# Recurrent heads summed onto all partitions and normalised one by one, with the attention halves of two output stages ahead of the head halves

## The reference, cut to what matters

```python
o = outs[0] + outs[1]                                          # forward + backward, (B, S, 4, 128)
o = o * rsqrt(mean(o * o, axis=-1) + EPS)                      # one mean per head and token
o_hgrn = o.reshape(B, S, 512) * norm_g * silu(g_raw)
mixed = concatenate([o_hgrn, o_attn], axis=-1) @ w_mix_out[l]  # 1024 -> 1024
x = x + g2[:, None, :] * mixed
h = modulate(rmsnorm(x, norm_g[l, 2]), sh3, sc3)               # then the second feed-forward
```

## Time and profile before

| | us |
|---|---|
| Median of 3 runs (lowest, highest) | 1129.79 (1128.75, 1131.01) |
| The profiled execution | 1127.93 |
| Its span in the trace | 1126.1 |
| Matmuls busy (TensorE) | 1084.9 |
| VectorE, ScalarE, GpSimd busy | 561.0, 400.4, 75.6 |
| Mean granted TensorE clock | 0.988 |

### The profile page before, as it was taken

One profiled execution on the slowest core, in us unless ns is written; L12 is line 12 of the kernel. 1 busy time (PEld: TensorE's weight loads), 2 busy tenths in 40 slices (PEclk: granted clock), 3 DMA queues, 4 the chain that ended last, 5 costly groups with the idle time before them and its releaser, 6 DMA issues.

```text
span 1126.1 us, 12577 instructions
## 1 busy us (share of the span) xinstructions
PE 1084.9 (96%) x5007; PEld 875.7 (78%) x5007; DVE 561.0 (50%) x616; ACT 400.4 (36%) x496; POOL 75.6 (7%) x52
## 2 busy tenths in 40 slices
PE   7699999999999998999998999999999999999998
PEld 4488888888888876778886678787888888888886
DVE  5945545454545587334439993477223222232323
ACT  5542324232222353224337775244212222132221
POOL 0000000000000174000000000083000000000000
PEclk9899999999999999999999999999999999999999
DMA  8854655554354542213320001123232322323212
GB/s 337 305 187 160 214 178 194 191 181 186 112 206 168 154 131 95 92 51 99 97 54 1 1 1 38 38 77 104 81 112 75 111 97 89 112 75 112 86 64 74
DMA packets 89480, 133.45 MB, mean 119 GB/s; under 512 B 10569, under 2 KB 73413, under 8 KB 89318
## 3 DMA queue, kind: packets, MB, share of 16 engines
q1 hardware_dynamic: 89208, 130.82, 34.2%
q10 hardware_dynamic: 238, 2.17, 0.5%
HBM read 128.78 MB, written 4.19 MB: 118 GB/s over the span
## 4 chain that ended last, share of the span: by engine, by line
PE 86%; DVE 6%; ACT 3%; issue 2%; POOL 2%; SPq 0%; DMA 0%; ACTq 0%; DVEq 0%; POOLq 0%
PE bank L1309 26%; PE bank L1310 26%; PE bank L1311 26%; PE bank L1651 1%; PE bank L1374 1%; POOL sq L545 1%; DVE h_lo L957 1%; DVE qp_both L1195 1%; DVE a_diag L1212 1%; POOL tmod L548 1%; ACT kc L802 1%; PE bank L1634 1%; PE bank L1393 1%; PE bank L1362 1%; ACT lg L777 1%
## 5 line engine op out<-in xcount | busy, mean ns | idle before, releaser
L1309 PE MATMUL bank<-h_hi,w_hi 128*128 128x512 f32 x960 | 379.7, 396 | 17.1 <-DVE h_lo L957 15.0
L1310 PE MATMUL bank<-h_lo,w_hi 128*128 128x512 f32 x960 | 377.2, 393 | 0.0
L1311 PE MATMUL bank<-h_hi,w_lo 128*128 128x512 f32 x960 | 376.8, 393 | 0.0
L888 DVE TENSOR_TENSOR w_lo<-w_raw,w_hi 128x2048 fp32r<-128x2048 f32 x83 | 192.5, 2320 | 301.7 <-ACT w_hi L577 301.7
L577 ACT ACTIVATE w_hi<-w_raw 128x2048 fp32r<-128x2048 f32 x83 | 158.9, 1915 | 483.6 <-PE bank L1311 483.6
L1309 PEld LDWEIGHTS bank<-h_hi,w_hi 128*128 128x128 f32 x960 | 182.5, 190 | 59.9 <-DVE w_lo L888 10.0
L1311 PEld LDWEIGHTS bank<-h_hi,w_lo 128*128 128x128 f32 x960 | 182.4, 190 | 38.7
L1310 PEld LDWEIGHTS bank<-h_lo,w_hi 128*128 128x128 f32 x960 | 182.2, 190 | 37.9 <-issue 0.5
L1309 PE MATMUL bank<-a_hi,w_hi 128*128 128x512 f32 x352 | 137.3, 390 | 0.0
L1311 PE MATMUL bank<-a_hi,w_lo 128*128 128x512 f32 x352 | 137.0, 389 | 0.0
L1310 PE MATMUL bank<-a_lo,w_hi 128*128 128x512 f32 x352 | 137.0, 389 | 0.0
(11 more groups left out here) (185 smaller groups left out, 872.2 us busy)
## 6 DMA issues: line engine op xcount, KB each, us to landing
w_raw<-in_w_ffn_in SPq DMA_DIRECT2D x44, 1024.0 KB, 5.1
ada<-in_w_ada SPq DMA_DIRECT2D x30, 1024.0 KB, 4.9
w_raw<-in_w_ffn_out SPq DMA_DIRECT2D x22, 1024.0 KB, 4.8
w_raw<-in_w_mix_in SPq DMA_DIRECT2D x11, 1024.0 KB, 5.0
ada_first<-in_w_ada SPq DMA_DIRECT2D x6, 1024.0 KB, 17.8
x_nat<-in_x SPq DMA_DIRECT2D x1, 2048.0 KB, 15.3
bias_shear<-rowpad ACTq DMA_DIRECT2D x1, 2048.0 KB, 10.2
w_raw<-in_w_mix_in SPq DMA_DIRECT2D x8, 256.0 KB, 4.3
```

Source lines behind the costliest of these rows:

```text
L888: ve.tensor_tensor(w_lo[n % 2][:], raw[n % 2][:], as_f32(w_hi[n % 2][:]), ALU.subtract).then_inc(wlo_done, 1)
L1309: te.matmul(out_ap, wh, xh, start=first, stop=False)
L1310: te.matmul(out_ap, wh, xl, start=False, stop=False)
L1311: return te.matmul(out_ap, wl, xh, start=False, stop=last)
```

## The change

Each head is now summed by a matmul with a 128x128 matrix of ones, so that the sum lands on all 128 partitions at once. Root, reciprocal and product are then done head by head on 128x512 tiles, and the spreading matmuls L1688 and the indicator `ind_h` with its GpSimd memsets are gone. The four sums are spread through TensorE's list. The attention halves of stages 0 and 1 both stand ahead of the head half of stage 0.

```diff
-    ind_h = at("ind_h", [P, 7], f32, take(28))
-    rth = at("rth", [4, TOK], f32, o_ada + 8 * KB)
-    rrh = at("rrh", [4, TOK], f32, o_ada + 10 * KB)
+    rto = at("rto", [P, HH, TOK], f32, o_ada + 8 * KB)
...
-            sp.wait_ge(pool_set, 6)
+            sp.wait_ge(pool_set, 5)
...
-            nc.gpsimd.memset(ind_h[:], 0.0).then_inc(pool_set, 1)
-            nc.gpsimd.memset(ind_h[:, 3:4], 1.0).then_inc(pool_set, 1)
...
     (ScalarE; in the loop over h, o_square(h - 1) now only for h = 1 and 2)
-            o_square(HH - 1)
-            a.wait_ge(oh_ss, 1)
-            sc.activation(rth[:], bank[4][0:HH, :], ACT.Sqrt, bias=eps_t[0:HH, :], scale=1.0 / P).then_inc(oh_rt, 1)
-            for h in range(HH):
-                a.wait_ge(oh_m, h + 1)
-                sc.activation(h_hi[:, h, :], z[:, Z_Q + h, :], ACT.Copy).then_inc(mx_hi, 1)
+            def o_root(h):
+                a.wait_ge(oh_ss, h + 1)
+                sc.activation(rto[:, h, :], bank[h][:], ACT.Sqrt, bias=eps_t[:], scale=1.0 / P).then_inc(oh_rt, 1)
+            def o_hi(h):
+                a.wait_ge(oh_m, h + 1)
+                sc.activation(h_hi[:, h, :], z[:, Z_Q + h, :], ACT.Copy).then_inc(mx_hi, 1)
+            o_root(0); o_square(2); o_root(1); o_square(3); o_hi(0)
+            o_root(2); o_hi(1); o_root(3); o_hi(2); o_hi(3)
...
     (VectorE; in the loop over h, o_scale(h - 1) now only for h = 1 and 2)
-            o_scale(HH - 1)
-            v.wait_ge(oh_rt, 1)
-            ve.reciprocal(rrh[:], rth[:]).then_inc(oh_rr, 1)
-            for h in range(HH):
-                v.wait_ge(oh_bc, h + 1)
-                v.wait_ge(o_scl, h + 1)
-                ve.tensor_tensor(z[:, Z_Q + h, :], z[:, Z_Q + h, :], bank[(5, 1, 2, 3)[h]][:], ALU.mult
-                                 ).then_inc(oh_m, 1)
-            for h in range(HH): (o_lo(h))
+            def o_inverse(h):
+                v.wait_ge(oh_rt, h + 1)
+                ve.reciprocal(rto[:, h, :], rto[:, h, :]).then_inc(oh_rr, 1)
+            def o_norm(h):
+                v.wait_ge(oh_rr, h + 1)
+                v.wait_ge(o_scl, h + 1)
+                ve.tensor_tensor(z[:, Z_Q + h, :], z[:, Z_Q + h, :], rto[:, h, :], ALU.mult).then_inc(oh_m, 1)
+            def o_lo(h):   (the subtraction of L1277, unchanged)
+            o_inverse(0); o_norm(0); o_scale(2); o_inverse(1); o_scale(3); o_norm(1); o_lo(0)
+            o_inverse(2); o_norm(2); o_lo(1); o_inverse(3); o_norm(3); o_lo(2); o_lo(3)
...
     (TensorE)
-            for h in range(HH):
-                values(h)
-                if h + 2 < HH:
-                    far2(h + 2)
-            for h in range(HH):
-                pe.wait_ge(o_sqd, h + 1)
-                ins = te.matmul(bank[4][0:HH, :], ind_h[:, 3 - h:7 - h], o_sq[:, h, :],
-                                start=(h == 0), stop=(h == HH - 1))
-            ins.then_inc(oh_ss, 1)
+            def o_sum(h):
+                pe.wait_ge(o_sqd, h + 1)
+                pe.wait_ge(o_scl, h + 1)
+                te.matmul(bank[h][:], ones[:], o_sq[:, h, :], start=True, stop=True).then_inc(oh_ss, 1)
+            values(0); far2(2); values(1); far2(3)
+            o_sum(0); values(2); o_sum(1); values(3); o_sum(2)
...
-            pe.wait_ge(o_scl, HH)
-            out_part(0, range(HH, DT))
-            pe.wait_ge(oh_rr, 1)
-            for h in range(HH):
-                te.matmul(bank[(5, 1, 2, 3)[h]][:], ident[0:HH, h:h + 1].to_broadcast([HH, P]), rrh[:],
-                          start=True, stop=True).then_inc(oh_bc, 1)
+            out_part(0, range(HH, DT), (0,))
+            o_sum(3)
+            out_part(0, range(HH, DT), (1,))
+            pe.wait_ge(wlo_done, N_MIXOUT + 2)
+            out_part(1, range(HH, DT))
             for m in range(M_MIXOUT):
-                if m:
+                if m >= 2:
                     pe.wait_ge(wlo_done, N_MIXOUT + m + 1)
+                    pe.wait_ge(x_upd[1], 2 * (m - 1))
                 for cc in range(2):
-                    if m:
+                    if m >= 2:
                         out_part(m, range(HH, DT), (cc,))
                     out_part(m, range(HH), (cc,)).then_inc((mx_out, stage_done)[cc], 1)
```

More of the change, by code:

```diff
@@ L320, in build @@
             "far1_mm", "far2_mm", "far_act", "far_dve"))
-        pv_mm, o_sqd, o_scl, oh_ss, oh_rt, oh_rr, oh_bc, oh_m = (sem(n) for n in (
-            "pv_mm", "o_sqd", "o_scl", "oh_ss", "oh_rt", "oh_rr", "oh_bc", "oh_m"))
+        pv_mm, o_sqd, o_scl, oh_ss, oh_rt, oh_rr, oh_m = (sem(n) for n in (
+            "pv_mm", "o_sqd", "o_scl", "oh_ss", "oh_rt", "oh_rr", "oh_m"))
         mx_hi, mx_lo, mx_out = sem("mx_hi"), sem("mx_lo"), sem("mx_out")
@@ L845, in _ @@
                               ).then_inc(far_act, 1)
-                if h >= 1:
+                if h >= 1 and h < HH - 1:
                     o_square(h - 1)
@@ L854, in _ @@
                     whi(N_MIXOUT + 1)
-            o_square(HH - 1)
-            a.wait_ge(oh_ss, 1)
-            sc.activation(rth[:], bank[4][0:HH, :], ACT.Sqrt, bias=eps_t[0:HH, :], scale=1.0 / P).then_inc(oh_rt, 1)
-            for h in range(HH):
+            def o_root(h):
+                a.wait_ge(oh_ss, h + 1)
+                sc.activation(rto[:, h, :], bank[h][:], ACT.Sqrt, bias=eps_t[:], scale=1.0 / P).then_inc(oh_rt, 1)
+            def o_hi(h):
                 a.wait_ge(oh_m, h + 1)
                 sc.activation(h_hi[:, h, :], z[:, Z_Q + h, :], ACT.Copy).then_inc(mx_hi, 1)
+            o_root(0)
+            o_square(2)
+            o_root(1)
+            o_square(3)
+            o_hi(0)
+            o_root(2)
+            o_hi(1)
+            o_root(3)
+            o_hi(2)
+            o_hi(3)
             for m in range(M_MIXOUT):
@@ L1278, in _ @@
                                  ).then_inc(mx_lo, 1)
+            o_inverse(0)
+            o_norm(0)
+            o_scale(2)
+            o_inverse(1)
+            o_scale(3)
+            o_norm(1)
+            o_lo(0)
+            o_inverse(2)
+            o_norm(2)
+            o_lo(1)
+            o_inverse(3)
+            o_norm(3)
+            o_lo(2)
+            o_lo(3)
             for m in range(M_MIXOUT):
@@ L1364, in ada_sum @@
                 ins.then_inc(ada_mm, 1)
-            pe.wait_ge(pool_set, 9)
+            pe.wait_ge(pool_set, 7)
             pe.wait_ge(vec_done, 1)
@@ L1656, in _ @@
             far2(1)
-            for h in range(HH):
-                values(h)
-                if h + 2 < HH:
-                    far2(h + 2)
-            for h in range(HH):
-                pe.wait_ge(o_sqd, h + 1)
-                ins = te.matmul(bank[4][0:HH, :], ind_h[:, 3 - h:7 - h], o_sq[:, h, :],
-                                start=(h == 0), stop=(h == HH - 1))
-            ins.then_inc(oh_ss, 1)
+            def o_sum(h):
+                pe.wait_ge(o_sqd, h + 1)
+                pe.wait_ge(o_scl, h + 1)
+                te.matmul(bank[h][:], ones[:], o_sq[:, h, :], start=True, stop=True).then_inc(oh_ss, 1)
+            values(0)
+            far2(2)
+            values(1)
+            far2(3)
+            o_sum(0)
+            values(2)
+            o_sum(1)
+            values(3)
+            o_sum(2)
             def out_part(m, tiles, halves=range(2)):
@@ L1683, in _ @@
             pe.wait_ge(o_lod, 1)
-            pe.wait_ge(o_scl, HH)
-            out_part(0, range(HH, DT))
-            pe.wait_ge(oh_rr, 1)
-            for h in range(HH):
-                te.matmul(bank[(5, 1, 2, 3)[h]][:], ident[0:HH, h:h + 1].to_broadcast([HH, P]), rrh[:],
-                          start=True, stop=True).then_inc(oh_bc, 1)
+            out_part(0, range(HH, DT), (0,))
[3 more added lines that the diff above has]
+            out_part(1, range(HH, DT))
             for m in range(M_MIXOUT):
-                if m:
+                if m >= 2:
                     pe.wait_ge(wlo_done, N_MIXOUT + m + 1)
+                    pe.wait_ge(x_upd[1], 2 * (m - 1))
+                for cc in range(2):
                     if m >= 2:
-                        pe.wait_ge(x_upd[1], 2 * (m - 1))
-                for cc in range(2):
-                    if m:
                         out_part(m, range(HH, DT), (cc,))
```

4 lines of the change are left out of this document (2 added, 2 removed).

## The result

| | before | after |
|---|---|---|
| Median of 4 runs each (lowest, highest) | 1129.35 (1128.75, 1131.01) | 1121.28 (1120.91, 1121.68) |
| The profiled execution | 1127.93 | 1121.30 |
| Its span | 1126.1 | 1119.5 |

The ratio is 0.9926, with a 95% interval of 0.9909 to 0.9944: the change makes the kernel faster, by 8.1 us at the medians. The two profiled executions differ by 6.6. The forecast was 1123.6, a gain of 6.2, with a range from 1121.4. The result lies just outside it, on the fast side. The forecast was counted from a median before of 1129.79; the table has one run more and 1129.35, so 0.4 of the 2.3 us between forecast and result is no part of the gain.

What follows compares the result with a forecast made beforehand. TensorE was taken as the bound: 5.08 + 1.9 - 0.3 = 6.7 us saved there, plus 0.05 at the start, less 0.5 behind stage 0, say 6.2. From the median of 1129.79 that gives 1123.6, range 1121.4 to 1126.8.

Steps and rivals of the forecast that it cites:

- What bounds the kernel: TensorE, busy 1084.9 of 1126.1 us; it waits 1.4 us for L1277 and 2.6 us for L957.
- Spreading and wait: Before stage 0's head half: the spreading matmuls and the wait behind them go, saving TensorE 5.08 us.
- Changes between kinds of matmul: TensorE's sums now split the attention half and stand between `values`: 0.3 us added, bounds 0 and 0.6.
- The low clock: Head half of stage 0: the clock at 0.53 cost 1.9 us, saved if no new gap comes.
- Why the clock fell: Head half of stage 0: the clock fell to the lower level after the four-row matmuls and the wait.
- Whether the heads are ready: VectorE's four reciprocals and the rest, 20.4 us, finish before TensorE needs the heads; margins 0.2 to 0.9 us, no wait.
- After stage 0: GpSimd's later work in the second feed-forward's norm may lengthen the wait at L957: 0.5 us lost, between 0 and 1.5.
- Start of the kernel: Removed memset L517 on the chain of the first microseconds: 0.05 us saved, bounds 0 and 0.1.
- Sum: Whole kernel: 6.7 + 0.05 - 0.5 = 6.25, say 6.2 us gained; time 1123.6 from the median of 1129.79.
- The reciprocals are late: Rival, 0.12: VectorE's queue slips 1.5 us, TensorE waits 1 us in stage 0's head half, clock falls; gain 3.3, time 1126.5.
- slower: Rival, 0.03: no reciprocal before the last sum, so stage 1 ends 5 us later than before; time 1135.
- GpSimd sets the end: Rival, 0.08: every tile of the second feed-forward's norm hangs on GpSimd; gain 4.2 to 5.2 us, time 1125.1.

Runs made afterwards that it cites:

- The move alone: Kernel before with its old normalisation, only stage 1's attention half moved behind the spreading matmuls, head 0's spread to bank 0: 1127.75 us, ratio to before 0.9981.
- the four-row against the 128-row matmuls: Changed kernel plus four unused f32 matmuls between stage 1's attention half and the head half: 1126.78 us reading four rows, 1125.03 us reading 128.
- The added reciprocal: Changed kernel plus one 128x512 reciprocal into a spare tile ahead of head 0's: 1125.13 us, 3.6 above the changed kernel.
- the first of the last two versions: Changed kernel, but in the second feed-forward's norm VectorE also makes tile 1 and GpSimd three tiles: 1121.34 us, ratio to before 0.9923.
- the normalisation alone: Changed kernel with the attention half of stage 1 put back in stage 1: 1127.86 us, ratio to before 0.9985.
- lighter GpSimd: Changed kernel with GpSimd's three folding adds ahead of the second feed-forward cut to two columns: 1120.80 us, ratio to before 0.9919.

## Why the prediction came out as it did

- **What bounds the kernel.** Right. The waits at L1277 and L957 were the two places, and the change acted on both.
- **Spreading and wait, 5.08.** Right: no such rows and no such wait afterwards.
- **Changes between kinds of matmul, -0.3.** Wrong in size. At the end of stage 1 the two profiles differ by 6.98, and the changed kernel had come there 0.19 us late already (its copy ahead of the sums starts at 691.53, against 691.34). That is 7.17, where 5.08 + 1.9 are 6.98; the term was +0.2, for each sum took 0.86 and left no gap.
- **The low clock, 1.9.** This is the step that failed, by the size of its term: "The low clock cost 7.43 - 5.44 - 0.1 = 1.9 us". That was true of the profiled execution and was carried to the median. Three profiles show 1.9, 2.9 and 2.8, so the typical term is some 0.9 larger, as far as three profiles tell. The hand-over in that sum was read too small as well: in the first profile the next stage's first matmul starts at 719.78, 0.26 before ScalarE and not 0.1. From start to start the three losses are 1.7, 2.7 and 2.6, which leaves their differences as they are and moves 0.2 to the term above. That the profiled run lay 1.9 under the median was in the table. The prediction added this as a constant to both kernels, though the changed one has no low clock at this place that could vary. The profile of the changed kernel lies at its own median.
- **Why the clock fell.** The prediction put it down to "the four-row matmuls and the wait". The move alone, and the four-row against the 128-row matmuls, show that the four-row ones are enough. The added reciprocal shows that a wait of 2.5 us can do it too, though the first of the last two versions kept a clock of 1.00 behind 2.58.
- **Whether the heads are ready.** Right. The margin is 0.5 us at sum 3 and at head 3 in the profile, and 0.9 at sum 2 by the added reciprocal; the prediction had 0.2 to 0.9 and gave none for sum 2. Without the moved half it is a loss of 4.5 us.
- **After stage 0.** The mechanism was right (GpSimd late against TensorE) and the price 0.3 against 0.5. Its form was not foreseen: the prediction kept 1.72 us for the first low part, which took 0.74. So the wait did not grow at the first tile but shrank there and came back at the next two, and the low clock in this norm went.
- **Start of the kernel, 0.05.** Not to be seen: the changed kernel is 0.19 us later by 691 us, within what executions of one kernel differ by there (0.45 among three profiles of before, 1.0 with those of the other versions).
- **Sum.** 6.25, plus 0.9 for the clock, 0.5 for the changes of kind and 0.2 for GpSimd, less 0.2 for the start, is 7.6, the difference of the median spans. Some 0.5 outside the span makes 8.1. Why the time around the span varies in the kernel before and not in the changed one was not found; the move alone shows it too (1.75 to 2.9), the normalisation alone does not (1.8).
- **The rivals.** "The reciprocals are late" and "slower" did not occur; the normalisation alone shows the first of them once the cover is gone. "GpSimd sets the end" is what the norm does now, at a price of 0.3 us. The reach of the range on the fast side, a gain of 7.0 and the scatter, lacked the error of the clock term.

## What to carry to other kernels

Work that delays TensorE's next product costs its own time, the wait behind it and the clock behind both; read the clock behind every thin or idle stretch, in more than one profile, since the same stretch lost 1.9 to 2.9 us here. When a profiled execution lies well under the median of the runs, ask which term of the sum makes the difference before it is added to both kernels. A serial chain may be made four times longer on an engine with room (here four reciprocals in place of one), as long as independent matmuls of the same length stand in front of what it feeds. Here that took both parts of the change: the two parts gave 1.8 and 1.9 us alone and 8.1 together.

## What the runs showed of the hardware

- Four f32 matmuls of 4x512 against 4x128 took 3.7 us, four of 128 rows 0.3 less. The former lowered the granted clock though TensorE never stood idle: 0.61 over the 3.6 us behind them, 1.00 behind the same number with 128 rows. Whether the few rows or the zeros in the fixed matrix do it is open.
- In one execution of the kernel before the clock fell while its four-row matmuls ran: 4.79 us in place of 3.70.
- The same wait of 2.58 us was followed by a granted clock of 0.79 in one version (lighter GpSimd) and of 1.00 in another (VectorE makes tile 1). Three waits of 0.98, 1.21 and 1.71 us in the changed kernel left it at 1.00.
- Beside GpSimd's scaling (L542, one tile as input) VectorE's instructions with two tiles as input took 0.75, 1.18 and 0.74 us, the last of them beside the start of a product as well. Those that began beside its products (two tiles; the lighter GpSimd) took 1.75 to 1.77. One scaling itself took 3.61 us, beside VectorE's subtraction of 128x2048, where the others took 1.6. The Trainium skill (SBUF — State Buffer, "Who interferes with whom") says that a VectorE instruction with two SBUF inputs contends with any GpSimd one that reads SBUF. The products agree with that, and so does the scaling of 3.61. The first low part does not (757.83, 0.74 us, beside L542 until 758.21); GpSimd's spans in a profile are rough, and why it was not held up stays open.
